# Token chunks 272 words apart, matmuls taken in groups of chunks, and weight halves placed alike modulo 256 bytes, in the first block of a two-block transformer kernel

## The chip, the core and the metric

One NeuronCore of a Trainium2 chip runs the whole kernel. The metric is the device time of one execution in microseconds (us). TensorE does the matrix products, VectorE (DVE) and ScalarE (ACT) the elementwise work, GpSimd (POOL) a few sums, and SyncE (SP) issues the weight transfers. All weights stream from HBM once.

## The reference, cut to what matters

Two stacks of two layers each run one after the other on 256 tokens (272 in the first stack, which has 16 extra ones in front). The first stack is "block one":

```python
for l in range(2):                       # block one, 272 tokens (256 at the end of its second layer)
    h = layer_norm(ALPHA * h + 0.5 * swiglu(h, ffn1...), ...)
    proj = h @ w_in[l]                   # 1024 -> 20 blocks of 128 columns
    mix = concat(ssd_mixer(...), fox_mixer(...), mla_mixer(...)) @ w_out[l]
    h = layer_norm(ALPHA * h + mix, ...)
    h = layer_norm(ALPHA * h + 0.5 * swiglu(h, ffn2...), ...)

def swiglu(x, w_gate, w_up, w_down):     # 1024 -> 2816 -> 1024
    return (silu(x @ w_gate) * (x @ w_up)) @ w_down
```

Block two has the same frame (RMS norm, two swiglu layers of the same size, an input projection, mixers, an output projection) on 256 tokens. Everything is float32.

## The kernel before

**Tiling.** Activations lie transposed: 128 of the 1024 features on the partitions, the tokens along them, so a tensor is 8 chunks (KD) of T columns, and the hidden layer 22 chunks (NF). A product with one block of 128 output features is a unit: for each of the chunks, 128x128 weights are loaded and T token columns stream past them into one PSUM bank. To keep float32 precision each operand is split into a high part, rounded to the fast format float32r, and the low rest. Each chunk then takes three matmuls: low weights with high tokens, high weights with low tokens, high weights with high tokens (the helper `three`, L612 to L618; `mm` at L616, L617, L618). A narrow unit has 8 chunks and 24 matmuls (`narrow_unit`, L620), a hidden unit, half of a block of the down projection, 11 chunks and 33 matmuls (`down`, L784).

**Weights.** SP loads pairs of units into `raw` (two slots j, two halves u: four units). ACT copies a unit to `w_hi`, DVE subtracts into `w_lo` (L1268, L1271, L1967), and PE waits for `lo_done`. All loops run through the four units (j, u) in turn.

**Places.** A LINE is 16 words, 64 bytes; 4 of them are 256 bytes. The buffers are allocated one behind the other with gaps that the kernel chooses. `Place(pitch, high, low)` says where the 8 chunks of a narrow unit lie: how far apart they are, and how far the first is shifted in `w_hi` and in `w_lo`. TIGHT is 128 words apart and no shift, OPENING is 128 apart with a shift of one line, BESIDE_274 and BESIDE_258 are 160 apart. The token chunks of 272 or 274 columns lie 288 words apart (X_PITCH), those of 256 columns 256 apart, the hidden chunks 272 (or 256) apart. Counted in lines modulo 4 from the start of `w_hi`, `w_lo` begins at 2, `x_hi_all` and `x_lo_all` at 3, `plain` at 1, `hid_hi` at 0 and `hid_lo` at 2.

**Stages of block one.** The first swiglu of layer one ("opening", `up` with opening=True, 272 columns), its `down` (272), `mixer1` with 20 input blocks of 274 columns (two columns more carry the norm's gain and bias) between the mixers' own small matmuls, `out_proj` (272), `level_up` with 274 columns from the buffer `plain`, `down` (272). Layer two is the same with `level_up` for its first swiglu; its output projection has 256 columns, its last `level_up` 258, its last `down` 256. `crossing_up` begins block two, with 258 columns in four units. From there on all is 256 columns, with TIGHT weights.

## Time and profile before

| | us |
|---|---|
| median of 3 runs (1950.46 to 1952.63) | 1950.91 |
| the profiled execution | 1950.55 |
| its span, first to last instruction | 1948.7 |
| TensorE matmuls busy | 1936.3 (99%) |
| TensorE weight loads busy | 1897.6 (97%) |
| VectorE busy | 1428.9 (73%) |
| ScalarE busy | 1019.9 (52%) |

A matmul row's own duration (some 0.28 us) is its way through the array. Matmuls overlap, so what a matmul costs is the distance from its start to the start of the next, called its **step** below. In a stretch without pauses it is the stretch, plus one matmul's duration since the count also holds the one that was under way at its beginning, divided by the count.

### The profile page before, as it was taken

The numbers are of one execution on the slowest core, as the hardware profiler recorded it, in microseconds if no ns is written. First come the engines' busy times: TensorE is split into PE (matmuls) and PEld (weight loads), VectorE is DVE, ScalarE is ACT, GpSimd is POOL, SyncE is SP. The second block draws the span as 40 slices with busy tenths as digits, with TensorE's granted clock in tenths as the row PEclk, the third lists the DMA queues.
The fourth block names the chain that finished last, engine by engine and source line by source line (L and its number), as shares of the span: only waits on it lengthen the run. The fifth ranks groups of instructions, "written<-read, shape, count | busy, mean of one in ns | idle before, by whom it ended". The sixth has DMA issues, their size and how long they took to land.

```text
span 1948.7 us, 42291 instructions
## 1 busy us (share of the span) xinstructions
PE 1936.3 (99%) x16150; PEld 1897.6 (97%) x16150; DVE 1428.9 (73%) x2591; ACT 1019.9 (52%) x1527; POOL 152.7 (8%) x192
## 2 busy tenths in 40 slices
PE   9999999999999999999999999999999999999998
PEld 9999989999999999899999999999999999999998
DVE  6774787887688768879878874667765775667763
ACT  4443687554455446865547443565445444565443
POOL 0001123000100011320010100000000000100000
PEclk9999999999999999999999999999999999999999
DMA  7454433545454544345553665435555555435554
GB/s 264 174 200 165 166 109 123 181 172 192 154 188 172 187 167 158 109 152 194 198 191 134 237 231 191 152 140 189 192 219 177 194 202 208 151 130 195 194 213 154
DMA packets 46830, 346.66 MB, mean 178 GB/s; under 512 B 5344, under 2 KB 6416, under 8 KB 9232
## 3 DMA queue, kind: packets, MB, share of 16 engines
q1 hardware_dynamic: 44416, 335.63, 47.7%
q0 software_dynamic: 2320, 9.74, 1.6%
q8 instruction: 63, 1.03, 0.2%
q14 instruction: 31, 0.25, 0.0%
HBM read 344.29 MB, written 1.07 MB: 177 GB/s over the span
## 4 chain that ended last, share of the span: by engine, by line
PE 91%; DVE 4%; ACT 2%; DVEq 1%; issue 1%; ACTq 0%; DMA 0%; SPq 0%; POOL 0%
PE ps L616 29%; PE ps L618 29%; PE ps L617 29%; DVE w_lo L1967 1%; PE ps L1133 0%; DVE pj L2429 0%; DVE cst L2450 0%; PE ps L1168 0%; DVE pj L2426 0%; ACT scratch L1640 0%; DVE scratch L2395 0%; PE ps L958 0%; DMA raw<-in_w_up 0%; PE ps L969 0%; ACT w_hi L1268 0%
## 5 line engine op out<-in xcount | busy, mean ns | idle before, releaser
L1967 DVE TENSOR_TENSOR w_lo<-raw,w_hi 128x1024 fp32r<-128x1024 f32 (+1 forms) x582 | 749.6, 1314 | 153.7 <-ACT w_hi L1271 91.2
L616 PE MATMUL ps<-x_hi,w_lo 128*128 128x256 f32 (+3 forms) x2416 | 685.2, 284 | 1.6 <-DVE x_lo L2058 0.7
L618 PE MATMUL ps<-x_hi,w_hi 128*128 128x256 f32 (+3 forms) x2416 | 676.1, 280 | 0.0
L617 PE MATMUL ps<-x_lo,w_hi 128*128 128x256 f32 (+3 forms) x2416 | 675.3, 280 | 0.0
L1268 ACT ACTIVATE w_hi<-raw 128x1024 fp32r<-128x1024 f32 x454 | 466.2, 1052 | 110.2 <-PE ps L618 91.5
L616 PEld LDWEIGHTS ps<-x_hi,w_lo 128*128 128x128 f32 x2416 | 454.9, 188 | 9.2 <-issue 5.7
L617 PEld LDWEIGHTS ps<-x_lo,w_hi 128*128 128x128 f32 x2416 | 454.6, 188 | 0.8
L618 PEld LDWEIGHTS ps<-x_hi,w_hi 128*128 128x128 f32 x2416 | 454.1, 188 | 0.0
L616 PE MATMUL ps<-hid_hi,w_lo 128*128 128x256 f32 (+1 forms) x1536 | 431.7, 281 | 0.0
L618 PE MATMUL ps<-hid_hi,w_hi 128*128 128x256 f32 (+1 forms) x1536 | 430.5, 280 | 0.0
L617 PE MATMUL ps<-hid_lo,w_hi 128*128 128x256 f32 (+1 forms) x1536 | 430.1, 280 | 0.0
L616 PE MATMUL ps<-plain,w_lo 128*128 128x274 f32 (+1 forms) x1088 | 313.4, 288 | 0.0
L618 PE MATMUL ps<-plain,w_hi 128*128 128x274 f32 (+1 forms) x1088 | 311.3, 286 | 0.0
L617 PE MATMUL ps<-plain,w_hi 128*128 128x274 f32 (+1 forms) x1088 | 310.3, 285 | 0.0
L616 PEld LDWEIGHTS ps<-hid_hi,w_lo 128*128 128x128 f32 x1536 | 288.8, 188 | 2.4 <-DVE hid_lo L2695 1.4
L618 PEld LDWEIGHTS ps<-hid_hi,w_hi 128*128 128x128 f32 x1536 | 289.0, 188 | 0.0
L617 PEld LDWEIGHTS ps<-hid_lo,w_hi 128*128 128x128 f32 x1536 | 288.5, 188 | 0.0
L617 PEld LDWEIGHTS ps<-plain,w_hi 128*128 128x128 f32 x1088 | 206.7, 190 | 0.3
L616 PEld LDWEIGHTS ps<-plain,w_lo 128*128 128x128 f32 x1088 | 205.9, 189 | 0.5 <-issue 0.2
L618 PEld LDWEIGHTS ps<-plain,w_hi 128*128 128x128 f32 x1088 | 204.3, 188 | 0.0
L1319 ACT ACTIVATE silu<-silu 128x256 f32<-128x256 f32 (+1 forms) x108 | 45.3, 420 | 274.6 <-DVE silu L1981 274.6
L1271 ACT ACTIVATE w_hi<-raw 128x1408 fp32r<-128x1408 f32 x128 | 169.0, 1368 | 2.9 <-PE ps L618 2.2
(331 smaller groups left out, 1584.5 us busy)
## 6 DMA issues: line engine op xcount, KB each, us to landing
raw<-in_w_up SPq DMA_DIRECT2D x176, 1024.0 KB, 4.8
raw<-in_w_down SPq DMA_DIRECT2D x64, 1408.0 KB, 6.0
raw<-in_w_in SPq DMA_DIRECT2D x36, 1024.0 KB, 4.8
raw<-in_w_out SPq DMA_DIRECT2D x16, 1024.0 KB, 4.8
cst<-row_copy POOLq DMA_DIRECT2D x2, 1088.0 KB, 8.8
raw<-in_w_up SPq DMA_DIRECT2D x4, 512.0 KB, 6.7
cst<-in_consts POOLq DMA_DIRECT2D x1, 1537.5 KB, 6.5
prm<-in_prm POOLq DMA_DIRECT2D x2, 690.0 KB, 7.1
```

The lines of the kernel that those rows point to most:

```text
L616: mm(dst, low, xa, start=first, stop=False)
L617: mm(dst, high, xb, start=False, stop=False)
L618: return mm(dst, high, xa, start=False, stop=last)
L1268: fn(narrow_at(w_hi, place, j, u), narrow_raw(j, u), ACT.Copy).then_inc(hi_done, 1)
L1271: fn(w_hi[:, j, c], raw[:, j, c], ACT.Copy).then_inc(hi_done, 1)
L1319: fn(silu[:, j, 0:T], silu[:, j, 0:T], ACT.Silu).then_inc(silu_done, 1)
L1967: v.tensor_tensor(dst, src, high.bitcast(F32), ALU.subtract).then_inc(lo_done, 1)
```

## The change

The token chunks of 272 columns are packed 272 words apart (they were 288), the 258-column ones in `plain` too; 274-column chunks stay 288 apart. The high and the low tokens begin at the same line modulo 4, in the buffers of `x`, of `plain` and of the hidden layer. Units are computed in groups of chunks instead of chunk by chunk: in a group first all low weights with high tokens, then all high weights with low tokens, then high with high. TOGETHER gives the group's size: 4 for 272 and 258 columns, 2 for 274, and 1 (the old order) for 256. In `down` with 272 columns the eleven chunks go in groups of 4, 4 and 3. The places of the narrow units change: weight chunks are 144 words apart beside tokens of 272 and 258 columns, 160 beside 274; the high and low halves of a unit begin at the same line modulo 4, and each of the four units (j, u) at another one. The number of matmuls, transfers, copies and waits stays as it was. The 256-column stages keep places and order.

```diff
-        PLAIN_LO = [KD * X_PITCH + n * LINE for n in (6, 6, 5, 6)]
-        PLAIN_AT, PLAIN_W = 640, max(PLAIN_LO) + KD * X_PITCH
+        PLAIN_AT, PLAIN_W = 640, 2 * KD * X_PITCH
...
-        x_hi, x_lo = chunks(x_hi_all[:, 2 * LINE:], KD, X_PITCH), chunks(x_lo_all, KD, X_PITCH)
+        x_hi, x_lo = chunks(x_hi_all, KD, X_PITCH), chunks(x_lo_all, KD, X_PITCH)
+        x1_hi, x1_lo = chunks(x_hi_all, KD, T1), chunks(x_lo_all, KD, T1)
         xt_hi, xt_lo = chunks(x_hi_all, KD, T2), chunks(x_lo_all, KD, T2)
-        hid_hi, hid_lo = chunks(hid_hi_all, NF, T1), chunks(hid_lo_all, NF, T1)
+        hid_hi, hid_lo = chunks(hid_hi_all[:, HID_HI_AT:], NF, T1), chunks(hid_lo_all[:, HID_LO_AT:], NF, T1)
...
+        def plain_of(T):
+            pitch = T1 if T == T2 else X_PITCH
+            return chunks(plain, KD, pitch), chunks(plain[:, KD * pitch:], KD, pitch)
...
-        TIGHT = Place(P, 0, 0)
-        OPENING = Place(P, LINE, LINE)
-        BESIDE_274 = Place(P + 2 * LINE, 2 * LINE, 0)
-        BESIDE_258 = Place(P + 2 * LINE, LINE, 0)
+        TIGHT = Place(P, (0, 0, 0, 0), (0, 0, 0, 0))
+        BESIDE_272 = Place(P + LINE, (0, 2, 1, 3), (2, 0, 3, 1))
+        BESIDE_274 = Place(P + 2 * LINE, (0, 2, 1, 3), (2, 0, 3, 1))
+        LEVEL_274 = Place(P + 2 * LINE, (2, 0, 3, 1), (0, 2, 1, 3))
+        LEVEL_258 = Place(P + LINE, (2, 0, 3, 1), (0, 2, 1, 3))
+        TOGETHER = {T1: 4, T1 + 2: 2, T2 + 2: 4, T2: 1}
...
-            a = u * W_WIDE + (place.low if buffer is w_lo else place.high)
+            a = u * W_WIDE + (place.low if buffer is w_lo else place.high)[2 * j + u] * LINE
...
+            def grouped(dst, high, low, xa, xb, T, n, together):
+
+                for k0 in range(0, n, together):
+                    group = range(k0, min(k0 + together, n))
+                    for w, x in ((low, xa), (high, xb), (high, xa)):
+                        for k in group:
+                            last = mm(dst, w[:, k, :], x[:, k, 0:T], start=w is low and k == 0,
+                                      stop=w is high and x is xa and k == n - 1)
+                return last
...
-                for k in range(KD):
-                    if k in before:
-                        before[k]()
-                    last = three(dst, high[:, k, :], low[:, k, :], xa[:, k, 0:T], xb[:, k, 0:T], k == 0, k == KD - 1)
+                if before or T not in TOGETHER:
...
+                else:
+                    last = grouped(dst, high, low, xa, xb, T, KD, TOGETHER[T])
...
+            def hidden_half(dst, j, u, ha, hb, T):
+
+                for c0 in range(0, HALF_F, TOGETHER[T]):
+                    group = range(c0, min(c0 + TOGETHER[T], HALF_F))
+                    for w, x in ((w_lo, ha), (w_hi, hb), (w_hi, ha)):
+                        for c in group:
+                            f, col = u * HALF_F + c, u * W_WIDE + c * P
+                            last = mm(dst, w[:, j, col:col + P], x[:, f, 0:T], start=w is w_lo and f == 0,
+                                      stop=w is w_hi and x is ha and f == NF - 1)
+                return last
...
-                            for c in range(HALF_F):
...
+                            if T == T1:
+                                last = hidden_half(ps[:, 4 + j, 0:T], j, u, ha, hb, T)
```

## Rows read from the trace of the kernel before

**Rows 1.** The page: busy share, and TensorE's granted clock in 40 slices.

```profile
PE 1936.3 (99%) x16150; PEld 1897.6 (97%) x16150; DVE 1428.9 (73%) x2591; ACT 1019.9 (52%) x1527; POOL 152.7 (8%) x192
PEclk9999999999999999999999999999999999999999
```

**Rows 2.** The cores: span and mean granted TensorE clock.

```profile
core 0: 1948.7 us, clock 0.999
```

**Rows 3.** The waits: PE's, longest in total first: us, times, longest.

```profile
PE ps L1228 <- DVE rstd L2762: 1.2, 1, 1.2
PE ps L1006 <- ACT scratch L1649: 0.7, 2, 0.4
```

**Rows 4.** Busy us by stretch (from:to, length): PE, PEld, DVE, ACT, POOL (counts), clock, DMA.

```profile
20.00:130.00 110.00, 110.00 (x891) 110.00 (x891) 80.49 (x134) 46.18 (x57) 1.23 (x2) 1.00 0.57 203
140.00:200.00 60.00, 60.00 (x483) 60.00 (x482) 27.21 (x26) 22.36 (x26) 9.08 (x12) 1.00 0.48 177
344.00:458.00 114.00, 114.00 (x894) 114.00 (x893) 97.51 (x195) 57.80 (x77) 0.00 (x0) 1.00 0.50 179
468.00:528.00 60.00, 60.00 (x483) 60.00 (x482) 37.64 (x47) 24.43 (x29) 9.03 (x12) 1.00 0.49 180
548.00:662.00 114.00, 114.00 (x910) 114.00 (x909) 96.93 (x194) 57.69 (x78) 0.00 (x0) 1.00 0.52 190
668.00:728.00 60.00, 60.00 (x483) 60.00 (x482) 37.59 (x47) 24.40 (x30) 9.04 (x12) 1.00 0.50 180
870.00:968.00 98.00, 98.00 (x827) 98.00 (x826) 87.92 (x179) 53.07 (x71) 0.00 (x0) 1.00 0.53 193
980.00:1036.00 56.00, 56.00 (x497) 56.00 (x496) 38.32 (x50) 24.41 (x29) 8.63 (x12) 1.00 0.52 193
1074.00:1164.00 90.00, 90.00 (x796) 90.00 (x796) 71.36 (x123) 42.00 (x53) 7.04 (x13) 1.00 0.66 231
```

**Rows 5.** Groups by line, first of each shape: count, busy us, mean ns.

```profile
L616 PE MATMUL ps<-x_hi,w_lo 128*128 128x256 f32 x1696 | 473.6, 279 | 1.5 <-DVE x_lo L2058 0.7 <-DVE w_lo L1967 0.6 <-DVE x_lo L2512 0.2
L616 PE MATMUL ps<-plain,w_lo 128*128 128x274 f32 x704 | 205.0, 291 | 0.0
L618 PE MATMUL ps<-hid_hi,w_hi 128*128 128x272 f32 x528 | 152.0, 288 | 0.0
L616 PE MATMUL ps<-x_hi,w_lo 128*128 128x272 f32 x400 | 115.1, 288 | 0.0
L617 PE MATMUL ps<-plain,w_hi 128*128 128x258 f32 x384 | 108.5, 283 | 0.0
L616 PE MATMUL ps<-x_hi,w_lo 128*128 128x274 f32 x272 | 82.4, 303 | 0.0
```

**Rows 6.** Timeline of PE in layer one's input projection: start, duration, instruction.

```profile
242.18 0.29 PE L617 MATMUL ps<-x_lo,w_hi 128*128 128x274 f32 x1
...
242.81 0.30 PE L616 MATMUL ps<-x_hi,w_lo 128*128 128x274 f32 x1
242.95 0.30 PE L617 MATMUL ps<-x_lo,w_hi 128*128 128x274 f32 x1
...
247.29 0.29 PE L618 MATMUL ps<-x_hi,w_hi 128*128 128x274 f32 x1
```

**Rows 7.** Timeline of PE there: twelve matmuls of plain float32, merged in one row.

```profile
230.56 2.99 PE L857 MATMUL ps<-scratch,prm 128*128 128x272 f32 x12
```

**Rows 8.** One line, L857: duration ns min/median/max, first and last start.

```profile
L857 PE MATMUL ps<-scratch,prm x12: 392/392/468, 230.6 to 233.2; 128*128 128x272 f32 x12
```

More of the change, by code:

```diff
@@ L624, in narrow_unit @@
                 pe.wait_ge(lo_done, turn * 4 + (2 * j + u + 1))
-                for k in range(KD):
-                    if k in before:
-                        before[k]()
-                    last = three(dst, high[:, k, :], low[:, k, :], xa[:, k, 0:T], xb[:, k, 0:T], k == 0, k == KD - 1)
+                if before or T not in TOGETHER:
+                    for k in range(KD):
+                        if k in before:
+                            before[k]()
+                        last = three(dst, high[:, k, :], low[:, k, :], xa[:, k, 0:T], xb[:, k, 0:T], k == 0, k == KD - 1)
+                else:
+                    last = grouped(dst, high, low, xa, xb, T, KD, TOGETHER[T])
                 last.then_inc(unit_used, 1)
@@ L654, in opening_pair @@
                     for u in range(2):
[L655 removed]
+                        step(w_hi, x1_hi, u, k, start=k == 0)
                 pe.wait_ge(head_lo, 2)
@@ L659, in opening_pair @@
                     for u in range(2):
-                        step(w_lo, x_hi, u, k)
-                        step(w_hi, x_lo, u, k)
+                        step(w_lo, x1_hi, u, k)
+                        step(w_hi, x1_lo, u, k)
                 pe.wait_ge(lo_done, 2)
@@ L665, in opening_pair @@
                     for u in range(2):
-                        step(w_lo, x_hi, u, k)
-                        step(w_hi, x_lo, u, k)
-                        last = step(w_hi, x_hi, u, k, stop=k == KD - 1)
+                        step(w_lo, x1_hi, u, k)
+                        step(w_hi, x1_lo, u, k)
+                        last = step(w_hi, x1_hi, u, k, stop=k == KD - 1)
                         if k == KD - 1:
@@ L688, in up @@
                             narrow_unit(turn0 + half * 2 + (1 + i // 2), j, u, ps[:, 2 * j + u, 0:T], T,
-                                        place=OPENING if opening else TIGHT)
+                                        place=BESIDE_272 if opening else TIGHT)
             def level_up(q, turn0, norm, T):
-                N, xs, place = T + 2, (plain_hi, plain_lo_of(LEVEL_NORM[norm])), level_place(T)
+                N, xs, place = T + 2, plain_of(T), level_place(T)
                 pieces = {5: lambda: mean(norm, T)}
@@ L1910, in _ @@
                 if l == 0:
-                    up(q, t0 + SEC1["ffn1"], T1, place=OPENING)
+                    up(q, t0 + SEC1["ffn1"], T1, place=BESIDE_272)
                 else:
```

47 lines of the change are left out of this document (23 added, 24 removed).

## The prediction

> **What bounds the kernel now.** I read the page first: PE is busy 99% of the span, its weight loads 97% [rows 1], at a granted clock of 0.999, the 2.4 GHz level [rows 2], and its longest wait is 1.2 us, before any real work [rows 3]. The chain that sets the end is PE's own stream, and a change that removes neither matmuls nor waits can act only through the step from one matmul to the next. The table by stretch gives it: length plus one duration of about 0.29 us (0.28 at 256 columns), divided by PE's count [rows 4].
>
> Opening, 272 columns: 110.29/891 = 123.8 ns. Down, 272 columns, three stages alike: 60.29/483 = 124.8. First level_up, 274 columns: 114.29/894 = 127.8. Second, same shape: 114.29/910 = 125.6. Level_up with 258 columns: 98.28/827 = 118.8. The 256-column stages: 56.28/497 = 113.2 and 90.28/796 = 113.4. Input projection, 274 columns: 40 steps from 242.18 to 247.29, 127.8 [rows 6].
>
> One column per clock takes N/2.4: 106.7 ns for 256 columns, 107.5 for 258, 113.3 for 272, 114.2 for 274. Above that the opening pays 10.5, down 11.5, the two level_ups 13.6 and 11.4, 258 columns 11.3, the input projection 13.6, but 256 columns only 6.7. **This is the number that matters:** two columns more are worth 0.8 ns and cost 5.4.
>
> **What is different about 256 columns?** From the places, in lines modulo 4: tokens always begin at 3, the weights at 0 (high) or 2 (low), so the distance of tokens from weights is 3 or 1. And 256 columns are exactly 16 lines, so each matmul begins in the line in which the one before would have gone on. Three stages test this today. Level_up with 274 columns has plain at 1 and 3, weights at 2, all moving by 2 a chunk: distances 3 and 1 too, and each matmul begins 14 words past where the last ended. It pays 11.4 to 13.6, so odd distance with a nearly unbroken run is not enough. Opening has tokens at 1 and 3, weights at 1 and 3, even distances, each matmul a whole line past the last one's end: 10.5. Even distance is thus not worse. In down the distance rotates and every third matmul goes on exactly: 11.5. What no stage but those of 256 columns has is the exact run from every matmul to the next.
>
> **The change, part by part.** Nothing is added to or removed from any queue: ACT and DVE write the same units to other offsets, SP's transfers and all waits are as before, and PE has all of a unit's weights and tokens before its first matmul. These edits cost nothing outside PE. The cover is DVE, busy 87.92 of 98 us in the 258-column stage [rows 4]. If the step there fell by 4.6 to 114.2, DVE's share would be 0.897 x 118.8/114.2 = 93%; PE would wait for w_lo only at a step under 0.897 x 118.8 = 106.6 ns. DMA moves 231 GB/s in a 256-column stage, more than the 180 to 203 it moves here.
>
> The matmuls touched, from the counts [rows 5] and the loops: opening 42 units of 24, 1008; down 3 x 528 = 1584; out_proj of layer one 144; placed units of level_up 960, 960 (274 columns) and 960 (258); placed input blocks 2 x 16 x 24 = 768; other grouped but TIGHT units some 220. In all some 6600 of 16150. The pairs that go chunk by chunk as tokens arrive and all 256-column stages stay.
>
> The new order is not in this trace, so a step is bounded. **Lower bound:** plain float32 matmuls of 272 columns with full weights run 12 in 2.99 us; without the last one's 392 ns and the 76 ns by which the first is longer, 11 steps take 2.52 us [rows 7, 8], 229 ns each, twice 113.3 plus 2.5. At 2.5 ns above N/2.4 the 6600 would save about 6600 x (11.7 - 2.5) = 61 us. **Nearest row:** the 256-column stages with 6.7 ns, the same format and the same three matmuls. Stage by stage: opening 3.8 x 1008 = 3.8; down 4.8 x 1584 = 7.6; out_proj at down's 4.8 x 144 = 0.7; level_up 6.9 x 960 = 6.6, 4.7 x 960 = 4.5 and 4.6 x 960 = 4.4; input projection 6.9 x 768 = 5.3; the rest 5 x 220 = 1.1. Sum 34 us. **Upper bound:** the longest step in the input projection without a wait, 242.81 to 242.95 [rows 6], some 135 ns, 8 above the mean of 127; all 6600 at that would cost 53 us.
>
> **Which value.** 272 columns packed 272 apart, in groups of four, are the exact run: 17 lines each, 68 a group, back to the first line. So opening and out_proj reach 6.7: 3.8 + 0.7 = 4.5 us. In down the last group has three chunks (51 lines, a line off at three of 33 steps), and the weights stay TIGHT while tokens move a line a chunk, so the distance still rotates: I give it half, 3.8 us. With 258 and 274 columns each matmul still begins 14 words past the last one's end, as 274 columns do now, and the distance goes from 3 and 1 to 3, 1, 2 or 0 by unit, of which the trace prefers none: nothing. Sum **8 us**: 1950.55 - 8.3 = 1942.3 against the profiled execution, which lies 0.4 under the median, so 1942.
>
> **A rule that speaks against it.** Steps of the same format pay 6.7 to 13.6 ns above N/2.4 in these rows. The Trainium skill, "TensorE: Matmul & The Clock Gate", section "Step-by-step: what each phase is for", says that TensorE has two independent SBUF read ports, and that loading the next weights takes no read bandwidth from the running matmul. By that rule places could do nothing, and the time would stay: the first rival below. The plain float32 rows [rows 8] agree with it, the jump between 256 and 258 columns does not.
>
> **The rivals.**
> *Nothing moves.* What separates 256 columns is their count, and order and place are worth a nanosecond either way. For it: stages with quite different places all pay 10.5 to 13.6, and two stages of 274 columns with the same places, order and shape differ by 2.2 ns [rows 4], which is no address. Down's one exact step in three has brought it nothing over opening. Against: 5.4 ns for two columns. Half a nanosecond either way on 6600 is 3.3 us: 1947 to 1954, around 1950.5.
> *Gain everywhere.* The distance held for a whole unit, or high and low alike, is what counts, and the 14 words don't matter: up to the 34 us, 1917, and at half that 1934. For it: today no stage but 256 columns keeps tokens and weights in a fixed pattern of lines together with an unbroken run. Against: the 274-column stages come close and pay most.
> *Slower.* A distance that is held for a whole unit can be the bad one in all its matmuls, while today it changes from one to the next and is averaged. The longest step, 8 ns above the mean, may be its price. If one of the four distances costs that, a quarter of the 4600 placed matmuls loses 1150 x 8 = 9 us, two of four lose 18. Against the 4 us of opening and down that would remain it is 1950.5 + 18 - 8 = 1960 with two, about 1952 with one; it decides as soon as two units in four lose more than 4 ns. Against: opening holds even distances, level_up odd ones, and neither stands out.
> *It doesn't do what it says.* If the lines are off by one somewhere, the exact run is broken at each change of the group, one step in four: some 2 us less than forecast, 1944, which is inside its range.
>
> **How the numbers follow.** Gain mostly at 272 columns, 4 to 14 us: 0.31 (own range 1936.5 to 1946.5, with 1944 in it). Gain everywhere, 14 to 40 us: 0.24, of which 0.07 lies under 1920. Nothing: 0.23. Slower: 0.22, of which 0.1 above 1958. The range leaves out these two tails: 1920 to 1958. A measurement of this kernel tells about 0.2%, 4 us, from no change: faster 0.55, same 0.23, slower 0.22.
>
> **What would show it.** In the table by stretch: opening at about 120 ns a step, down at 122, the 274- and 258-column stages within 1 ns of now, the 256-column stages unchanged at 113.3. In the timeline of a level_up, four units in turn of 24 steps each: if they differ, distance matters, and which unit is long says which distance is bad. If the 274-column stages fall to 121, the second rival holds; if opening stays at 124, the first. PE's waits should stay near nothing. The prediction fails if a stage's step grows beyond 130, or if DVE's w_lo begins to release PE.

## The result and the profile after

The changed kernel takes 1954.92 us (median of 18 runs, 1954.70 to 1955.42), the kernel before, run in turn with it, 1950.57 us (18 runs, 1948.30 to 1952.72). The ratio is 1.0025, with a 95% interval of 1.0018 to 1.0031: slower by 4.4 us. That lies inside the range of 1920 to 1958, on the other side of no change than the forecast of 1942. Note the spreads: before covers 4.4 us and its times lie in three heaps (near 1948.5, 1950.6 and 1952.7), after covers 0.7 us. The section on one arrangement with two steps says what makes the heaps.

The page, the cores and PE's longest waits of the changed kernel, in the views of [rows 1 to 3]:

```profile
PE 1939.8 (99%) x16150; PEld 1901.3 (97%) x16150; DVE 1428.9 (73%) x2591; ACT 1021.1 (52%) x1527; POOL 152.9 (8%) x192
core 0: 1952.9 us, clock 0.999
PE ps L1256 <- DVE rstd L2791: 1.2, 1, 1.2
PE ps L663 <- ACT x_hi L1928: 0.8, 1, 0.8
```

As many matmuls, the same clock, DVE, ACT and POOL as busy as before, and no wait of PE over 1.2 us. The span grew by 4.2 us and PE's busy time by 3.5. So the question stays the one of the prediction: which steps changed. The table by stretch of the changed kernel, columns as in [rows 4]: opening, down, the two level_ups of 274 columns, that of 258, down with 256 columns, a 256-column stage.

```profile
20.00:130.00 110.00, 110.00 (x879) 110.00 (x878) 79.66 (x133) 45.40 (x57) 1.23 (x2) 1.00 0.54 198
142.00:202.00 60.00, 60.00 (x480) 60.00 (x479) 26.96 (x24) 22.01 (x27) 9.06 (x12) 1.00 0.48 175
344.00:458.00 114.00, 114.00 (x903) 114.00 (x902) 98.22 (x196) 59.46 (x79) 0.00 (x0) 1.00 0.50 179
550.00:664.00 114.00, 114.00 (x903) 114.00 (x903) 96.02 (x194) 56.86 (x77) 0.00 (x0) 1.00 0.52 188
870.00:968.00 98.00, 98.00 (x814) 98.00 (x813) 86.92 (x178) 52.79 (x70) 0.00 (x0) 1.00 0.54 193
984.00:1036.00 52.00, 52.00 (x461) 52.00 (x460) 35.91 (x48) 20.84 (x21) 7.21 (x10) 1.00 0.53 191
1074.00:1164.00 90.00, 90.00 (x796) 90.00 (x795) 72.01 (x123) 41.95 (x55) 7.07 (x13) 1.00 0.66 232
```

Steps, worked out as in the prediction (length plus one duration, divided by PE's count), before against after:

| stage | columns | before | after | whole stage, first to last start, after minus before |
|---|---|---|---|---|
| opening | 272 | 123.8 | 125.5 | +1.6 us |
| down, three stages | 272 | 124.8 | 125.6 | +0.4 each |
| level_up, first | 274 | 127.8 | 126.6 | -1.2 |
| level_up, second | 274 | 125.6 | 126.6 | +0.9 |
| level_up, 258 | 258 | 118.8 | 120.7 | +1.8 |
| down and x, 256 | 256 | 113.2 to 113.4 | 113.4 | +0.1 |

With out_proj (+0.1) and the input projections (-0.2 in all) this makes the 4.2 us, within what the rounding allows. Three things are to be seen. The two level_ups of equal shape, which differed by 2.2 ns [rows 4], now agree. 258 columns, which had the shortest step of the touched stages, lost most. And nothing came near the 120 ns that the prediction put on the packed 272 columns.

The chain that ended last of the changed kernel shows the same with whole stages as single pieces (start, us, what):

```profile
14.07 126.47 PE ps L627 x1008
140.54 66.40 PE ps L805 x528
339.38 127.56 PE ps L627 x1008
864.53 119.05 PE ps L627 x984
```

126.47/1008 = 125.5, 66.40/528 = 125.8, 127.56/1008 = 126.5, 119.05/984 = 121.0: within each of these pieces PE has no idle time from the first to the last matmul.

In the opening and in level_up each unit (j, u) has its own distance of tokens from weights, in lines modulo 4: 3, 1, 2 and 0 in the order (0, 0), (0, 1), (1, 0), (1, 1). The loop over the placed units begins with (0, 0). Timeline of PE in the 258-column stage, the start of each of these four units and of the next (0, 0):

```profile
925.41 0.64 PE L627 MATMUL ps<-plain,w_lo 128*128 128x258 f32 x4
...
928.33 0.65 PE L627 MATMUL ps<-plain,w_lo 128*128 128x258 f32 x4
...
931.25 0.63 PE L627 MATMUL ps<-plain,w_lo 128*128 128x258 f32 x4
...
934.09 0.66 PE L627 MATMUL ps<-plain,w_lo 128*128 128x258 f32 x4
...
937.01 0.64 PE L627 MATMUL ps<-plain,w_lo 128*128 128x258 f32 x4
```

Three units take 2.92 us for 24 steps, the one at distance 2 takes 2.84. The median of a unit's mean step, over the stage, in ns:

| distance, unit | opening, 272 | level_up, 274 (both stages) | level_up, 258 |
|---|---|---|---|
| 3, (0, 0) | 125.9 | 126.8 | 121.5 |
| 1, (0, 1) | 125.5 | 127.7 | 121.7 |
| 2, (1, 0) | 124.0 | 125.5 | 118.3 |
| 0, (1, 1) | 126.3 | 126.1 | 121.9 |

Seen one by one, the steps of a unit repeat. With 274 columns they go 126, 128, 125, 128, 126, 127 in unit (0, 0), 129, 133, 121 in (0, 1) and 128, 121, 128 in (1, 0). So there are patterns of a few steps, and place does matter: the unit at distance 2 is about as short as the better figures of the kernel before (123.8, 125.6, 118.8), the other three are longer. The experiments ask in which way place matters.

### The profile page after: what moved, and what is told of

Read it like the earlier page. It is cut to its first block, busy times and chain, and to the rows that moved or that the text cites. A ratio compares the mean times of both kernels' runs of the same rounds, so it can differ in the third digit from the quotient of the medians.

```text
span 1952.9 us, 42331 instructions
## 1 busy us (share of the span) xinstructions
PE 1939.8 (99%) x16150; PEld 1901.3 (97%) x16150; DVE 1428.9 (73%) x2591; ACT 1021.1 (52%) x1527; POOL 152.9 (8%) x192
## 4 chain that ended last, share of the span: by engine, by line
PE 91%; DVE 4%; ACT 2%; DVEq 1%; issue 1%; ACTq 0%; DMA 0%; SPq 0%; POOL 0%
PE ps L627 58%; PE ps L805 10%; PE ps L617 6%; PE ps L618 6%; PE ps L619 6%; DVE w_lo L1996 1%; PE ps L1161 0%; DVE pj L2458 0%; DVE cst L2479 0%; PE ps L1196 0%; DVE pj L2455 0%; ACT scratch L1669 0%; DVE scratch L2424 0%; PE ps L986 0%; PE ps L997 0%
## 5 line engine op out<-in xcount | busy, mean ns | idle before, releaser
L627 PE MATMUL ps<-x_hi,w_lo 128*128 128x256 f32 (+3 forms) x2232 | 558.0, 282 | 0.6 <-DVE w_lo L1996 0.6
L627 PE MATMUL ps<-x_hi,w_hi 128*128 128x256 f32 (+3 forms) x2232 | 552.2, 280 | 0.0
L627 PE MATMUL ps<-x_lo,w_hi 128*128 128x256 f32 (+3 forms) x2232 | 552.0, 280 | 0.0
L1296 ACT ACTIVATE w_hi<-raw 128x1024 fp32r<-128x1024 f32 x454 | 466.4, 1053 | 117.2 <-PE ps L627 97.3
L627 PE MATMUL ps<-plain,w_hi 128*128 128x274 f32 (+1 forms) x2032 | 322.2, 287 | 0.0
L627 PEld LDWEIGHTS ps<-plain,w_hi 128*128 128x128 f32 x2032 | 280.1, 190 | 0.0
L617 PE MATMUL ps<-hid_hi,w_lo 128*128 128x256 f32 x912 | 253.1, 278 | 0.0
L619 PE MATMUL ps<-hid_hi,w_hi 128*128 128x256 f32 x912 | 251.8, 276 | 0.0
L618 PE MATMUL ps<-hid_lo,w_hi 128*128 128x256 f32 x912 | 251.8, 276 | 0.0
L627 PE MATMUL ps<-plain,w_lo 128*128 128x274 f32 (+1 forms) x1016 | 194.7, 286 | 0.0
L619 PEld LDWEIGHTS ps<-hid_hi,w_hi 128*128 128x128 f32 x912 | 171.2, 188 | 0.0
```

The lines of the kernel that those rows point to most:

```text
L617: mm(dst, low, xa, start=first, stop=False)
L618: mm(dst, high, xb, start=False, stop=False)
L619: return mm(dst, high, xa, start=False, stop=last)
L627: last = mm(dst, w[:, k, :], x[:, k, 0:T], start=w is low and k == 0, stop=w is high and x is xa and k == n - 1)
L1296: fn(narrow_at(w_hi, place, j, u), narrow_raw(j, u), ACT.Copy).then_inc(hi_done, 1)
```

## The experiments

### The step measured by itself

A stage of the kernel holds one arrangement at a time, with DVE, ACT and transfers beside it. So the first experiment leaves the kernel as it was and appends blocks of matmuls behind its end, when the other engines are idle; its time (2157.02 us) is only that of a longer program. A block is 72 matmuls in the order low, high, high, with places, widths and order of its own, behind 3 matmuls of 32 columns that separate it:

```diff
+            pe.wait_ge(probe_data, 2)
+            for config in PROBES:
+                probe(*config)
...
+                    for k0 in range(0, KD, 1 if order == "three" else order):
+                        group = range(k0, k0 + (1 if order == "three" else order))
+                        for w, x in ((low, xa), (high, xb), (high, xa)):
+                            for k in group:
+                                mm(ps[0:wcols, 0, 0:n], w[:, k, 0:wcols], x[:, k, 0:n], ...)
```

> The kernel before with 22 blocks of 72 extra matmuls behind its end, each block 3 units of 8 chunks in one shape, with nothing else running; its time is longer by their 190 us and only their steps are read. Blocks 1 to 7: 240, 250, 256, 258, 264, 270, 272 columns, chunks packed to whole lines, tokens at line 3, weights TIGHT at 0 and 2, chunk by chunk. Blocks 8 and 9: 256 columns at chunk distances 272 and 288. Blocks 10 to 12: 256 columns, tokens at lines 0, 1, 2. Block 13: high and low weights both at 0. Blocks 14 to 17: 272 columns packed, groups of four, weight chunks 144 apart, distance 3, 1, 2, 0. Blocks 18 and 19: the same chunk by chunk, distance 3 and 2. Blocks 20 and 21: 272 columns with weights of 64 and of 32 columns. Block 22: 256 columns with weights of 64. Theory A (place: 256 columns are cheap since each matmul goes on in the line where the last ended): 256 columns at 272 or 288 apart rise from 113.3 ns to 117 or more, 272 columns packed in groups fall to about 120. Theory B (count: the weight load of 128 columns covers 256 tokens and anything longer pays): 256 columns stay at 113.3 at every chunk distance and line, 240 and 250 columns stay at 113.3 too or fall by no more than their columns, 258 jumps to 119, and 272 stays at 124 to 126 in every order. Theory C (the two streams collide in the same line): weights of 64 and 32 columns bring 272 columns down toward 116, by both theories' own terms only C says so.

Timeline of PE in two of its blocks (start, duration, instruction): 256 columns, chunks 256 apart, second and last start; then 256 columns, chunks 272 apart.

```profile
1977.25 0.28 PE L1294 MATMUL ps<-x_lo,w_hi 128*128 128x256 f32 x1
...
1985.19 0.28 PE L1294 MATMUL ps<-x_hi,w_hi 128*128 128x256 f32 x1
...
2021.75 0.28 PE L1294 MATMUL ps<-x_lo,w_hi 128*128 128x256 f32 x1
...
2029.93 0.28 PE L1294 MATMUL ps<-x_hi,w_hi 128*128 128x256 f32 x1
```

70 steps in 7.94 us are 113.4 ns, and in 8.18 us 116.9: the same matmuls, only the chunks elsewhere. All blocks (mean step in ns, without the first dozen):

| columns | arrangement | step |
|---|---|---|
| 256 | as in the kernel | 113.3 |
| 256 | tokens moved on by 1, 2, 3 lines | 119.2, 113.3, 118.3 |
| 256 | both weight halves at the same line | 117.8 |
| 256 | chunks 272 apart, 288 apart | 117.2, 118.2 |
| 240, 250 | chunks 240, 256 apart | 112.2, 117.8 |
| 258, 264, 270, 272 | chunks 272 apart | 121.0, 121.1, 124.4, 125.7 |
| 272 | groups of four, weights 144 apart, distance 3, 1, 2, 0 | 125.9, 125.6, 123.8, 125.7 |
| 272 | the same places chunk by chunk, distance 3, 2 | 124.3, 125.0 |
| 272 | chunks 272 apart, weights of 64, of 32 columns | 124.5, 124.4 |
| 256 | as in the kernel, weights of 64 columns | 113.3 |

The blocks show the kernel's own steps with no other engine at work, so neither DVE nor transfers make them. The blocks of 272 in groups of four are the changed kernel's arrangement: 124 to 126, not 120. They also give the opening's units one by one: 125.9, 125.6, 123.8 and 125.7 at distances 3, 1, 2 and 0, against 125.9, 125.5, 124.0 and 126.3 in the stage. The blocks move the tokens and the kernel moves the weights, so with both halves alike it is the distance between them that counts, to within 0.6 ns. And the amount of weights is hardly it either: with 64 or 32 columns of them 272 columns take 1.2 ns less than the 125.7 of the same arrangement with 128, and 256 columns the same 113.3. What remains is that 113.3 is narrow: an even distance, equal halves or moving lines each end it, even at 256 columns.

The second set of blocks (2307.08 us) separates moving lines from length.

> The kernel before with 37 blocks of 72 extra matmuls behind its end; only their steps are read. Weight halves are two lines apart, as in the kernel before. Blocks 1 to 4: 272 columns with chunks 320 apart, so that every matmul begins at the same line (3, 1, 0, 2), though the run of tokens is broken. Blocks 5 to 7: 258, 274, 256 columns 320 apart, line 3. Theory F (a fixed pattern of first lines is what 256 columns have): 272 at odd distance falls to 120, 258 to 114, 274 to 121. Theory G (the unbroken run is needed too): 124, 119 and 127 as now, only 256 columns reach 113.3. Block 8: 256 columns 272 apart, weights 144 apart, the distance held while the lines move: 113.3 if the distance is what counts, 117 if the lines must stand still. Blocks 9 to 14: 272 columns packed, weights 144 apart, distances 3, 1, 0, 2 chunk by chunk and 3, 0 in groups of four: F and G give 124 to 126, the prediction's distance theory 120 for odd ones. Blocks 15 to 20: 274 columns 288 apart, weights 160, distances 3, 1, 0, 2, and 3, 0 in groups of two: 125 to 128. Blocks 21 to 24: 258 columns 272 apart, weights 144: 117 to 122. Blocks 25 to 34: the same weights and tokens in every matmul, 128 to 512 columns, line 3: 6.7 ns above N/2.4 if the rest comes from changing lines, else 11 to 13 where the columns are no multiple of 64. Blocks 35 to 37: the same with 272 columns, lines 1, 0, 2.

Timeline of PE, 272 columns with chunks 320 apart, so that every matmul begins at the same line modulo 4; second and 72nd start.

```profile
1960.62 0.29 PE L1314 MATMUL ps<-x_lo,w_hi 128*128 128x272 f32 x1
...
1969.33 0.29 PE L1314 MATMUL ps<-x_hi,w_hi 128*128 128x272 f32 x1
```

8.71 us for 70 steps: 124.4 ns, and 125.5, 124.5 and 126.1 from the other three lines. Standing still does not bring 272 columns down. 256 columns with the distance held but the lines moving take 120.6, while at 320 apart, which is the same line modulo 4 again, they take 113.3. 272 packed with weights 144 apart and the halves two lines apart, distances 3, 1, 0, 2: 125.0, 126.1, 127.3, 127.2. 274 at 288 and 160 apart: 126.0 to 128.8; 258 at 272 and 144: 118.3 to 120.5. So 113.3 needs all of it: 256 columns, lines that stand still, an odd distance, halves two lines apart.

The last blocks repeat one matmul with the same weights and tokens. PE merged by the timeline:

```profile
2179.17 8.23 PE L1307 MATMUL ps<-x_hi,w_hi 128*128 128x128 f32 x72
2195.52 8.31 PE L1307 MATMUL ps<-x_hi,w_hi 128*128 128x240 f32 x72
2203.76 8.73 PE L1307 MATMUL ps<-x_hi,w_hi 128*128 128x256 f32 x72
2260.15 17.04 PE L1307 MATMUL ps<-x_hi,w_hi 128*128 128x512 f32 x72
```

128 and 240 columns take the same, 111.7 and 112.0 ns a step: a floor that the tokens don't set. 256 columns take 117.8, 272 123.4 (125.3 to 126.7 from the other three lines), 512 233.4. The excess over N/2.4 is 11 ns at 256 columns, 10 to 13 from 258 to 320, and 20 at 512, so it is no fixed cost for each matmul. The expectation gave 256 columns 6.7 ns above N/2.4 if the rest comes from changing lines. They pay 11 with nothing changing, so one pair repeated is not the 113.3 pattern either.

To see whether the kernel obeys what the blocks show, one edit moves the tokens of all x stages of 256 columns on by one line, and nothing else:

```diff
-        xt_hi, xt_lo = chunks(x_hi_all, KD, T2), chunks(x_lo_all, KD, T2)
+        xt_hi, xt_lo = chunks(x_hi_all[:, LINE:], KD, T2), chunks(x_lo_all[:, LINE:], KD, T2)
```

> The kernel before with the 256-column tokens of x, high and low, moved by one line, so that their distance from the weights is even (0 or 2) instead of odd. About 5000 matmuls of block two, the output projection of layer two of block one included, stream them. If the 113.3 ns of 256 columns hang on first lines, as the probe behind the kernel's end had it (113.3 odd, 118.3 and 119.2 even), their steps rise to 118 to 119 and the time by 25 to 29 us to 1975 to 1980, while the 256-column down stages, whose tokens lie elsewhere, stay at 113.3. If the count of columns makes them cheap, nothing changes: 1950.6.

1976.07 us (two runs), ratio 1.0135 (1.0115 to 1.0155). The table by stretch, an x stage and a down stage of 256 columns:

```profile
1074.00:1160.00 86.00, 86.00 (x725) 86.00 (x724) 64.18 (x108) 37.68 (x47) 7.07 (x13) 1.00 0.62 216
1172.00:1226.00 54.00, 54.00 (x479) 54.00 (x478) 26.54 (x24) 21.77 (x24) 4.45 (x6) 1.00 0.53 194
```

86.28/725 = 119.0 ns where the tokens moved, 54.28/479 = 113.3 where they didn't. 64 bytes cost 5.7 ns a matmul and 25 us in all. The first rival, by which places do next to nothing, is refuted for 256 columns. The clean figure of 113.3 was the right place to look, but it hangs on the combination, and the blocks of 272 columns show that no part of it which the change brings lowers their step to 120.

### The two halves of the change, one at a time

The changed kernel with its places but the old order, chunk by chunk:

```diff
-                if before or T not in TOGETHER:
+                if True:
...
-                            if T == T1:
+                            if False:
```

> The changed kernel with the old order: every chunk's three matmuls in a row, in the narrow units and in down; packing, lines and unit places stay changed. If the grouping made it slower, the steps return to the kernel before: opening 123.8, down 124.9, 274 columns 125.6 to 127.8, 258 columns 118.9, time 1950.6. If the places did, the steps stay at 126.2, 125.8, 126.7 and 121.2 and the time at 1955.

And the kernel before with its places, but the new order (`grouped` and `hidden_half` as in the change, with the same TOGETHER):

```diff
+        TOGETHER = {T1: 4, T1 + 2: 2, T2 + 2: 4, T2: 1}
...
+                else:
+                    last = grouped(dst, high, low, xa, xb, T, KD, TOGETHER[T])
```

> The kernel before with the new order alone (groups of 4, 2 and 4 chunks, down in 4, 4 and 3); packing, lines and places as before. If the grouping made it slower, 1955 and the steps of the changed kernel; if the places did, 1950.6 and the old steps. If neither alone does, both runs lie near 1950.6 and the loss belongs to the pair.

New places alone: 1954.73 us, ratio 1.0023 (1.0013 to 1.0032). New order alone: 1956.51, ratio 1.0034 (1.0021 to 1.0046). In the table by stretch, new places alone, opening and 258 columns; below it new order alone, opening, the first level_up, 258 columns:

```profile
20.00:130.00 110.00, 110.00 (x879) 110.00 (x878) 79.00 (x132) 45.44 (x57) 1.23 (x2) 1.00 0.54 198
870.00:968.00 98.00, 98.00 (x816) 98.00 (x815) 87.16 (x180) 52.73 (x71) 0.00 (x0) 1.00 0.53 193
```

```profile
20.00:130.00 110.00, 110.00 (x879) 110.00 (x878) 78.92 (x131) 45.52 (x57) 1.23 (x2) 1.00 0.55 198
344.00:458.00 114.00, 114.00 (x895) 114.00 (x894) 97.29 (x194) 59.05 (x79) 0.00 (x0) 1.00 0.50 179
870.00:968.00 98.00, 98.00 (x816) 97.84 (x816) 87.35 (x178) 52.54 (x72) 0.00 (x0) 1.00 0.52 186
```

The opening goes to 125.5 either way (110.29/879), down too, 258 columns to 120.4 (98.28/816). With the new order alone both stages of 274 columns take 127.7 (114.29/895), with the new places alone 126.7. Neither run came out as it had to if one of the halves carried the loss: each costs as much as both together, or more. With the new order alone all four units take 125.5 ns in the opening, 127.8 with 274 columns and 120.0 with 258. With the new places alone they differ again, but the unit at distance 2 is no longer short in the opening (125.3, against 124.5 at distance 3) or with 274 columns (127.8, against 125.8 at distances 3 and 1). So the step belongs to a pair of place and order. The old pairs were good ones, each half of the change alone leaves them, and the two halves together have a pair as good in one unit of four.

### Is the step a property of the distance?

If a unit's step in the changed kernel belongs to its distance, and not to what the units beside it do, then four units at one distance should all have that step. The kernel before, with level_up alone grouped, `plain` packed and alike as in the change, and all units placed as unit (0, 0) of the changed kernel:

```diff
+        LEVEL_274 = Place(P + 2 * LINE, 2 * LINE, 0)
+        LEVEL_258 = Place(P + LINE, 2 * LINE, 0)
+        TOGETHER = {T1 + 2: 2, T2 + 2: 4}
```

> The kernel before, with only the placed units of the three level_up stages changed, and all four units at the one distance at which unit 0 of the changed kernel ran: plain packed and alike as in the change, groups of 2 (274 columns) and 4 (258), weights 160 and 144 apart with both halves at line 2. Theory (the four units' steps in the changed kernel, 125.5 and 118.3 for unit 0, belong to the distance): steps 125.5 in both 274-column stages and 118.3 in the 258-column one, in every execution alike, so 1948 and without the spread of 4 us of the kernel before. Rival (a unit's step depends on what the units beside it do, or on the start of the stage): steps as in the kernel before or the mean of the changed one, 126.7 and 121, 1950 to 1953.

1953.45 us, ratio 1.0017 (1.0007 to 1.0026). First level_up and 258 columns; below them the starts of three units in a row of the 258-column stage:

```profile
344.00:458.00 114.00, 114.00 (x902) 114.00 (x901) 97.74 (x195) 58.66 (x78) 0.00 (x0) 1.00 0.51 180
870.00:968.00 98.00, 98.00 (x808) 98.00 (x807) 86.25 (x177) 52.04 (x71) 0.00 (x0) 1.00 0.52 188
```

```profile
926.49 0.65 PE L629 MATMUL ps<-plain,w_lo 128*128 128x258 f32 x4
...
929.41 0.65 PE L629 MATMUL ps<-plain,w_lo 128*128 128x258 f32 x4
...
932.33 0.65 PE L629 MATMUL ps<-plain,w_lo 128*128 128x258 f32 x4
```

114.29/902 = 126.7 and 98.28/808 = 121.6. The expectation has 125.5 and 118.3, but it takes these for the steps of unit (0, 0), and they are those of (1, 0). Unit (0, 0) itself has 126.8 and 121.5 in the changed kernel, and all four units now take this step, 126.7 and 121.7, in the same patterns (126, 128, 125, 128, 126, 127 with 274 columns), whatever stands beside them. Two blocks of 274 columns in this arrangement, in the last set below, take 126.7 as well. So in these arrangements a unit's step goes with its place and order, and not with its neighbours. All units at distance 2 were not run. As an estimate from the steps of unit (1, 0), the three stages would be 1.1, 1.1 and 3.2 us shorter than in this run, and the kernel would take 1948.0 us, which is no more than the shortest executions of the kernel before already show.

### One arrangement, two steps

One thing the place does not explain. In the kernel before, two stages with the same places, order and shape took 127.8 and 125.6 [rows 4]. The next set of blocks (2213.18 us) takes the before kernel's own arrangements in turn, a dozen times each (256 columns four times), entered behind other blocks and 3 to 15 separators:

```diff
+            for i, config in enumerate(PROBES):
+                probe(*config)
+                for n in range(3 + i % 13):
+                    mm(ps[0:32, 1, 0:32], w_hi[:, 0, 0:32], x_hi_all[:, 0:32], start=True, stop=True)
```

> The kernel before with 40 blocks of 48 extra matmuls behind its end; only their steps are read. Four arrangements take turns, each exactly as a stage of the kernel before has it: 274 columns of level_up, 258 columns of level_up, 272 columns of the opening (12 blocks each) and 256 columns (4 blocks). What changes from one block to the next of a kind is only how it is entered: 3 to 15 small matmuls lie between. Theory L (a stage falls into one of several repeating patterns of steps at its start and keeps it; in the traces 274 columns stand at 125.67 or 127.67 and 258 at 118.67 or 121.17): the 12 blocks of a kind show these values and perhaps others, with no values between, and the 256-column ones 113.3 always. Rival N (the spread comes from the other engines' traffic): with these idle all 12 blocks of a kind are alike.

Timeline of PE in two blocks of 274 columns with equal places and order, second and last start of each:

```profile
1961.28 0.29 PE L1317 MATMUL ps<-x_lo,w_hi 128*128 128x274 f32 x1
...
1967.17 0.29 PE L1317 MATMUL ps<-x_hi,w_hi 128*128 128x274 f32 x1
...
2110.77 0.28 PE L1317 MATMUL ps<-x_lo,w_hi 128*128 128x274 f32 x1
...
2116.54 0.29 PE L1317 MATMUL ps<-x_hi,w_hi 128*128 128x274 f32 x1
```

46 steps in 5.89 us (128.0) and in 5.77 us (125.4). Over their last 24 steps the twelve blocks of 274 columns take 127.8 eight times and 125.5 or 125.6 four times, nothing between; the steps repeat as 129, 129, 126 in the one kind and 126, 129, 122 or 126, 124, 127 in the other. 258 columns: 118.9 nine times, 121.1 three times. The opening's arrangement: 124.0 and 123.7 five times each, once 123.4 and once 125.5. 256 columns: 113.3 each time. Same code, same addresses, idle neighbours: which pattern the stream falls into depends on how it is entered, and then it stays to the block's end.

The kernel's own stages do the same. The first level_up and the 258-column one, in the part of two of these kernels that is the kernel before, unchanged; first the kernel of the first set of blocks, then that of this one:

```profile
344.00:458.00 114.00, 114.00 (x910) 114.00 (x909) 99.18 (x198) 60.13 (x80) 0.00 (x0) 1.00 0.51 181
```

```profile
344.00:458.00 114.00, 114.00 (x894) 114.00 (x894) 97.37 (x194) 58.03 (x77) 0.00 (x0) 1.00 0.53 179
870.00:968.00 98.00, 98.00 (x811) 98.00 (x810) 86.72 (x179) 52.54 (x71) 0.00 (x0) 1.00 0.55 190
```

125.6 against 127.8 ns in the first level_up, and 121.2 in the 258 columns against the 118.8 of [rows 4]. A stage of about 1000 such matmuls in the longer pattern costs some 2.1 us more, which is the distance of the heaps of the kernel before. The traces bear this out. From the end of the opening to the 15001st matmul, a part that seven traces have in common (but for the places of out_proj in the run of the searched opening), the kernel takes 1669.5 and 1670.0 us where both the first level_up and the 258-column stage are short, 1671.4 and 1671.5 where one of them is long, and 1673.4 to 1673.5 where both are (three traces). The second level_up was in the shorter pattern in all seven. The 4.4 us by which the changed kernel is slower are against the middle heap; against the shortest they are 6.4 us.

### Are there better arrangements?

Two more sets of blocks, 48 matmuls each, look through places and orders: 98 blocks, then 136 (2573.09 and 2822.91 us). An entry is columns, distance of token chunks, line of the high tokens, distance of weight chunks, shifts of high and low weights, size of the groups, columns of weights, line of the low tokens from the high, and repeats.

```diff
+PROBES = [
...
+    (272, 288, 1, 144, 0, 1, 4, 128, 0, 2),
...
+                probe(*config)
```

> The kernel before with 98 blocks of 48 extra matmuls behind its end; only their steps are read. Blocks 1 to 3: 320, 384 and 512 columns, block 4: 288 columns, with the pattern of the 256-column stages (line 3, weights TIGHT, halves two lines apart). If the pattern locks for every whole number of 4 lines, they step at 17/16 of a clock per column, 141.7, 170 and 226.7 ns, and 288 columns at more than 130. Then 50 arrangements of 272 columns, 22 of 274 and 22 of 258, drawn at random over chunk distance (272 or 288), line of the high tokens, of the low ones, of each weight half, weight distance (128, 144, 160) and order (chunk by chunk, groups of 2 or 4). If a placement can bring 272 columns to the 6.7 ns above N/2.4 that the prediction counted on, some of the 50 lie near 120; if not, all lie between 123 and 128, those of 258 columns between 118 and 122 and those of 274 between 125 and 129.

> The kernel before with 136 blocks of 48 extra matmuls behind its end; only their steps are read. Blocks 1 to 48: the down stages' shape (272 columns packed, weights TIGHT) for all 16 pairs of lines of high and low tokens, each chunk by chunk and in groups of 2 and 4. Blocks 49 to 88: 40 more arrangements of 272 columns, 288 apart, weights 144 or 160 apart. Blocks 89 to 136: 24 arrangements of 274 columns, weights 160 apart, each twice and entered differently. If the change's lines and groups for down were merely one draw among many, the 48 lie between 123.5 and 127 with the changed kernel's (both at line 3, groups of 4) near 125.8 and the kernel before's (lines 0 and 2, chunk by chunk) at 124.9, and none reaches 120. Of 274 columns some arrangements differ between their two entries by about 2 ns and some don't; one that stays at 125.6 or lower both times would make the level_ups steady.

272 columns in 50 arrangements: 122.8 to 127.2, half of them between 124.7 and 125.5. 22 of 274: 125.5 to 128.3. 22 of 258: 118.9 to 122.3. 320, 384 and 512 columns, which are whole multiples of 256 bytes as 256 are: 145.5, 173.3 and 231.8, or 12, 13 and 18 above N/2.4. In the second set 272 as in down: 124.4 to 126.2; 272 with chunks 288 apart: 123.3 to 126.1; 274 from two entries: 125.5 to 130.0, most alike at both entries, some not (125.5 and 127.8, 127.8 and 130.0). None of some 140 arrangements of 272 columns comes near the 120 of the forecast. These figures are means of the last 24 steps. The expectation of 17/16 of a clock a column for 320, 384 and 512 (141.7, 170 and 226.7) missed. Timeline of the best one, merged: chunks 288 apart, all tokens at line 0, low weights at line 3 and high at 0, groups of four.

```profile
2049.00 0.65 PE L1375 MATMUL ps<-x_lo,w_hi 128*128 128x272 f32 x4
...
2053.91 0.65 PE L1375 MATMUL ps<-x_hi,w_hi 128*128 128x272 f32 x4
```

40 steps in 4.91 us: 122.8 ns. The kernel before with its opening so arranged, and nothing else:

```diff
+        x1_hi, x1_lo = chunks(x_hi_all[:, LINE:], KD, X_PITCH), chunks(x_lo_all[:, LINE:], KD, X_PITCH)
-        OPENING = Place(P, LINE, LINE)
+        OPENING = Place(P + LINE, 0, LINE)
...
+                if place is OPENING:
+                    last = grouped(dst, high, low, xa, xb, T, KD, 4)
```

> The kernel before with the opening's 40 placed units in the arrangement that was fastest of 50 behind the kernel's end, at 122.8 ns a step: high and low tokens both at line 0 and 288 words apart, weight chunks 144 apart, high half at line 0, low half at line 3, groups of four chunks. If a step measured alone carries over, the opening's 960 placed matmuls go from 123.9 to 122.8, 1.1 us less, below what the times can tell. If the pattern depends on how a unit is entered, the opening lies anywhere from 122.8 to 126, up to 2 us more. Everything else is as before.

1949.72 us against 1950.71, ratio 0.9993 (0.9983 to 1.0002): not to be told from none by the time, but by the table by stretch:

```profile
20.00:130.00 110.00, 110.00 (x898) 110.00 (x897) 81.16 (x135) 46.13 (x57) 1.23 (x2) 1.00 0.56 206
```

110.29/898 = 122.8 ns, the block's figure to the tenth, in all four units, with DVE, ACT and transfers beside it. Blocks behind the end thus forecast this stage. The last kernel takes that and other arrangements for down, level_up and the input blocks, for 274 columns one that kept its short pattern from both entries:

```diff
-        PLAIN_LO = [KD * X_PITCH + n * LINE for n in (6, 6, 5, 6)]
+        PLAIN_LO = [KD * X_PITCH + n * LINE for n in (8, 8, 5, 6)]
-        hid_hi, hid_lo = chunks(hid_hi_all, NF, T1), chunks(hid_lo_all, NF, T1)
+        hid_hi, hid_lo = chunks(hid_hi_all, NF, T1), chunks(hid_lo_all[:, LINE:], NF, T1)
+            return chunks(plain[:, 2 * LINE if T == T1 else 0:], KD, X_PITCH)
-        BESIDE_274 = Place(P + 2 * LINE, 2 * LINE, 0)
+        BESIDE_274 = Place(P + 2 * LINE, LINE, 0)
+        LEVEL_274 = Place(P + 2 * LINE, 3 * LINE, 2 * LINE)
```

> The kernel before, old order outside the opening, with the fastest steady arrangement from the probes in each stage of block one. Opening as in e9 (122.8 ns a step). Down with 272 columns: low tokens one line further, lines 0 and 3 (124.4 instead of 124.9: 0.7 us). The two level_ups of 274 columns: high tokens at line 3, low ones at 1, weights at 3 and 0 (125.54 at both entries behind the end; in the kernel before 125.67 or 127.67 by execution, so 1.1 us less on the mean of each). The placed input blocks: the same distances, all two lines on, by moving the high weights from line 2 to 1 (up to 1 us). The 258-column stage is left alone and keeps its two patterns, 118.67 and 121.17. If steps measured behind the end carry over, the sum is 1.1 + 0.7 + 0 to 4.2 + up to 1 us: 1946 or 1948.5 by the 258-column stage's pattern, against 1948.3 to 1952.7, a ratio near 0.998, and no execution above 1949.5. If a pattern depends on its surroundings more than on its arrangement, 1949 to 1952 with a spread as before.

1947.34 us (11 runs, 1947.08 to 1947.97) against 1950.52, ratio 0.9985 (0.9976 to 0.9994). Opening, down, both level_ups, 258 columns:

```profile
20.00:130.00 110.00, 110.00 (x897) 110.00 (x897) 80.97 (x136) 46.16 (x57) 1.23 (x2) 1.00 0.55 204
142.00:202.00 60.00, 60.00 (x484) 60.00 (x483) 27.45 (x28) 23.19 (x31) 9.06 (x12) 1.00 0.45 161
344.00:458.00 114.00, 114.00 (x910) 114.00 (x909) 97.46 (x197) 57.84 (x77) 0.00 (x0) 1.00 0.52 186
548.00:662.00 114.00, 114.00 (x910) 114.00 (x910) 96.61 (x194) 59.07 (x78) 0.00 (x0) 1.00 0.50 182
870.00:968.00 98.00, 98.00 (x827) 98.00 (x826) 87.89 (x179) 53.54 (x72) 0.00 (x0) 1.00 0.54 197
```

123.0, 124.6, 125.6 and 125.6, 118.8. It is faster than both kernels, if by little, and every one of its runs lies below every run of the kernel before. The expectation had 1946 or 1948.5, and it came between them. In the traces it is 2.8 us shorter than the kernel before. The first level_up gives 2.2 of it, since in the trace before it stood in the longer pattern, the opening 0.5, and the three down stages 0.4 (a block had 124.4 ns a step, the stages take 124.7); the input projection of layer two gives 0.3 back. Against the shortest executions of the kernel before, 1948.5 us, the gain is 1.2 us. No run of it shows a stage in the longer pattern. Its 258-column stage keeps the arrangement that showed two patterns, so that none of 11 runs has an outlier says only that it was entered alike in them.

## Why the prediction was wrong

**What bounds the kernel** held: no new wait, no new idle time, the same clock, and the whole difference is in the steps of PE.

**Nothing outside PE** held. DVE's cover was not touched, since the 258-column step went up to 120.7, not down to 114.2. The 256-column stages stayed at 113.4.

**The failed step** is "what no stage but those of 256 columns has is the exact run from every matmul to the next", and with it "272 columns packed 272 apart, in groups of four, are the exact run, so opening and out_proj reach 6.7". The rows held seven stages and two sets of figures, 6.7 and 10.5 to 13.6; of the many things in which 256 columns differ from the rest I took the one that the change brings. The blocks took them apart. 256 columns a line on have the run from every matmul to the next (in lines modulo 4) as before, and cost 119.2. 272 columns with the run cost 124 to 126, and 320, 384 and 512 columns, which can have it with lines standing still, pay 12 to 18 ns. It may be a condition (256 columns lose their 113.3 when it is broken), but it brings nothing by itself. The forecast for opening was 120, measured 125.5; for down 122, measured 125.6. The terms of -4.5 and -3.8 us became +1.7 (opening and out_proj) and +1.2.

**"Nothing" for 258 and 274 columns** was right only for the sum of the 274-column stages, which moved by -1.2 and +0.9 us, and wrong in its ground. The prediction let the distance go to 3, 1, 2 or 0 by unit, "of which the trace prefers none". The changed kernel does prefer one: distance 2 takes 125.5 ns at 274 columns and 118.3 at 258, the others 126.1 to 127.7 and 121.5 to 121.9. 258 columns lost 1.8 us by it. I read their 11.3 ns of excess as the general level. It was one of the lowest figures that the shape has: 118.9 at best in the search and 122.3 at worst, with 118.3 in the second set of blocks and in unit (1, 0). The opening's 123.8 was likewise near the good end of the 122.8 to 127.2 of 272 columns, and down's 124.9 near that of the 124.4 to 126.2 of its own shape. Where a stage stands already near the good end of what its shape shows, a new arrangement drawn without a reason that holds loses, and the trace of before could not show where the ends are. That is the general fault of the sum: its bounds came from other shapes (113.3 at 256 columns), not from other arrangements of the same one.

**The rival "nothing moves"** used that two equal stages differ by 2.2 ns, "which is no address". That was half right: it is no address, it is one arrangement with two patterns. It should have warned more strongly, since steps that come from how a stream is entered can't be summed from places at all.

**The rival "slower"** had the sign, nearly the time (1952 with one bad distance) and a part of the mechanism: a distance that is held for a whole unit has a step of its own. But it had one or two bad distances at 8 ns each. The runs show one good distance, and three that are longer than it by 0.6 to 3.6 ns. The worst unit has 127.7 ns, some 1 over the mean of its stage. Nor is a held distance the whole of it, since the new order alone, with the old distances, costs 6.0 us. That its time came near is partly luck. Its sum also takes off 8 us of gain where its sentence says that 4 would remain.

**The rule on the read ports** (the Trainium skill, "TensorE: Matmul & The Clock Gate", "Step-by-step: what each phase is for": two independent ports, and loading weights takes no bandwidth from the running matmul). The runs divide it. That loading takes nothing from the running matmul agrees, or nearly: with half the weights 113.3 ns at 256 columns as with all, and 124.5 against 125.7 at 272. That the two are independent, places included, as the first rival took it, is contradicted by 5.7 ns a matmul for 64 bytes. The rows of the weight loads in the blocks last 189 ns with 128 columns of weights, 134 with 64 and 109 with 32, so that 64 columns more add 55 ns. The Trainium skill, "TensorE: Matmul & The Clock Gate", section "LDWEIGHTS (loading the stationary operand)", gives a load P/1.2, as an estimate 106.7 ns for 128 columns and 53.3 for 64. The trace agrees with the growth and not with the whole row. The floor of 111.7 ns under the short matmuls lies 5 ns above the estimate for 128 columns and may be that load, but no run here shows it as such: short matmuls with fewer weights were not run.

**Open.** What in the chip makes the patterns was not found. The places of tokens and weights modulo 256 bytes change the step, but no rule that I formed gave the figures of 272 columns, nor why distance 2 is the good one in groups and, with 272 and 274 columns, not chunk by chunk. All units at distance 2 were not run. Nor is it known what chooses the pattern at the entry of a stage, or whether the 258-column stage of the last kernel would show its longer one in more runs.

## What to carry to other kernels

When PE is never idle, compare steps (start to start) stage by stage, and over several executions, before a difference of 2% in one stage is put down to anything in the code. To choose places or an order, append blocks of matmuls in the candidate arrangements behind the kernel's end and read their steps: here they gave the steps of the last kernel's opening and level_up to the tenth of a nanosecond, and those of its down stages and of the changed kernel's units within 0.6, which no reasoning from other shapes did. When a loop runs through several places, read the steps place by place, and count from the loop's first pass which is which. Prefer an arrangement that gives the same step however it is entered over one that is sometimes shorter.

## What the hardware showed

- 64 bytes in the place of the tokens change the step of a 256-column matmul of this format from 113.3 to 119.0 ns, 25 us over the kernel.
- Weights and tokens held the same, steps of 128 to 240 columns all take 111.7 to 112.0 ns; from 256 on they grow faster than N/2.4 (117.8 at 256, 233.4 at 512).
- In groups of chunks, with both weight halves and both token halves alike, the distance of tokens from weights modulo 256 bytes goes with the step: 118.3 ns at two lines and 121.5 to 121.9 at the other three with 258 columns, 124.0 and 125.5 to 126.3 with 272. Neighbouring units at other distances don't change it (126.8 and 126.7 ns with 274 columns).
- One arrangement can have two steady steps, 125.5 and 127.8 ns (274 columns), 118.9 and 121.1 (258), with no other engine at work. Which it takes is settled when it is entered, and two such stages make executions of one kernel 2.1 us apart.
